# Re-ordered queues around latent attention, and the second block's scores as three products of rounded parts

## The reference, cut to what matters

```python
h = x
for i in range(2):
    h = h + (mla_mixer if i == 0 else gla_mixer)(rms_norm(h, ...))
    h = h + peer_ffn(rms_norm(h, ...), ...)
# second block, on rms_norm of h:
#   eight "neighbourhood" heads a (queries, keys, values of 64 each) and eight
#   "window" heads b with two key/value heads; q and k are rms-normed per head
s = einsum('qd,kd->qk', q, k) * 64 ** -0.5 + bias      # 256 x 256 per head
o = softmax(s) @ v                                      # heads b with a sink
h = h + (sigmoid(gate_a) * (o_a @ w_a) + sigmoid(gate_b) * (o_b @ w_b)) @ w_out
h = h + ffn(rms_norm(h))
```

## Time and profile before

| | |
|---|---|
| median of 3 runs | 2199.15 us (2199.08 to 2201.77) |
| profiled execution, its own time | 2194.29 us |
| its span, first to last instruction | 2192.6 us |
| PE busy | 2155.4 us, 98% of the span |
| DVE, ACT, POOL busy | 1555.7, 1246.0, 701.0 us |
| mean granted PE clock | 0.996 of full |
| latent attention | from 0 to about 135 us |
| second block up to its first scores | about 1808 to 1868 us |
| its 16 heads | 1868 to 1953 us |

### The profile page before, as it was taken

How to read it: one execution, slowest core, us unless ns; L and a number is a source line. 1 busy time by engine, 2 the same in 40 slices (tenths; PEclk the granted TensorE clock), 3 DMA queues, 4 the chain that set the end, 5 groups by cost and what they waited for, 6 DMA issues and landing times. The chain is left out here.

```text
span 2192.6 us, 35528 instructions
## 1 busy us (share of the span) xinstructions
PE 2155.4 (98%) x13161; PEld 1876.8 (86%) x13161; DVE 1555.7 (71%) x2944; ACT 1246.0 (57%) x2463; POOL 701.0 (32%) x340
## 2 busy tenths in 40 slices
PE   8899999999999999999999999999999999999999
PEld 8789998888888888887999888888888888887888
DVE  7658978888666666666698788866666669457776
ACT  6554577777455444564446777755545555555443
POOL 3217977777000000001698777720000004000000
PEclk9999999999999999999999999999999999999999
DMA  5144655555555555553555555555565557435554
GB/s 164 54 158 157 197 176 166 164 164 165 191 193 194 196 194 194 161 168 107 174 192 183 164 164 165 165 182 195 195 193 193 192 163 241 124 99 165 191 192 153
DMA packets 122956, 375.34 MB, mean 171 GB/s; under 512 B 13200, under 2 KB 18064, under 8 KB 122784
## 3 DMA queue, kind: packets, MB, share of 16 engines
q1 hardware_dynamic: 122352, 372.69, 52.6%
q10 hardware_dynamic: 432, 0.37, 0.0%
HBM read 371.96 MB, written 1.05 MB: 170 GB/s over the span
## 5 line engine op out<-in xcount | busy, mean ns | idle before, releaser
L250 ACT ACTIVATE hi<-raw 128x1024 fp32r<-128x1024 f32 (+2 forms) x705 | 738.0, 1048 | 365.9 <-PE bank L1424 113.6
L259 DVE TENSOR_TENSOR lo<-raw,hi 128x1024 fp32r<-128x1024 f32 (+2 forms) x445 | 537.3, 1211 | 266.0 <-ACT hi L250 265.6
L259 POOL TENSOR_TENSOR lo<-raw,hi 128x1024 fp32r<-128x1024 f32 (+1 forms) x260 | 628.9, 2423 | 222.4 <-ACT hi L250 222.0
L1465 PE MATMUL bank<-hi,pe_mh 128*128 128x512 f32 x1016 | 395.9, 390 | 1.3 <-DVE pe_ml L1719 1.3
L1466 PE MATMUL bank<-hi,pe_ml 128*128 128x512 f32 x1016 | 395.3, 389 | 0.0
L1413 PE MATMUL bank<-xx,hi 128*128 128x512 f32 x1176 | 308.9, 401 | 0.0
L1578 ACT ACTIVATE pe_mh<-pe_hidden 128x256 fp32r<-128x256 f32 x256 | 106.9, 418 | 341.9 <-PE bank L1472 341.9
L342 POOL TENSOR_TENSOR rstd<-mean,minus_half 128x2 f32<-128x2 f32 x6 | 4.2, 703 | 920.8 <-DVE mean L335 920.8
L1424 PEld LDWEIGHTS bank<-xx,lo 128*128 128x128 f32 x2048 | 269.4, 188 | 13.9
L1424 PE MATMUL bank<-xx,lo 128*128 128x256 f32 x2048 | 280.5, 280 | 0.0
L1472 PE MATMUL bank<-lo,pe_mh 128*128 128x512 f32 x1016 | 271.6, 389 | 0.0
(11 more groups left out here) (404 smaller groups left out, 3372.0 us busy)
## 6 DMA issues: line engine op xcount, KB each, us to landing
raw<-in_peer_u SPq DMA_DIRECT2D x256, 512.0 KB, 3.3
raw<-in_peer_v SPq DMA_DIRECT2D x256, 512.0 KB, 3.4
raw<-in_w_gate_up SPq DMA_DIRECT2D x44, 512.0 KB, 3.7
raw<-in_w_in SPq DMA_DIRECT2D x34, 512.0 KB, 4.4
raw<-in_gla_w_in SPq DMA_DIRECT2D x24, 512.0 KB, 3.6
raw<-in_w_down SPq DMA_DIRECT2D x22, 512.0 KB, 3.4
raw<-in_w_query SPq DMA_DIRECT2D x16, 512.0 KB, 3.3
raw<-in_mla_w_o SPq DMA_DIRECT2D x8, 512.0 KB, 3.3
```

The lines of the kernel that those rows point to most:

```text
L250: act.activation(k.hi[:, n % RING, at_hi:at_hi + x * e], k.raw[:, n % RAW, 0:x * e], ACT.Copy).then_inc(k.hi_done, 1)
L259: eng.tensor_tensor(k.lo[:, n % RING, at_lo:at_lo + x * e], k.raw[:, n % RAW, 0:x * e], k.hi[:, n % RING, at_hi:at_hi + x * e].bitcast(F32 ...
L1465: pe.matmul(second_ps(a, c), mh[:, v % 2, tok], hi[:, r, half], start=(v == 0), stop=False)
```

## The change

The diff is cut to what matters; the parts left out repeat those shown. In the latent attention, queues are re-ordered: DVE takes the sum, the mean and the copies of x before the angles, ACT copies x before it splits slab 0, fewer warming products run, POOL makes the low part of slab 3, `gain_rows` moves behind the low part of slab 6, POOL's turning of the mask goes behind its slabs 8 and 9, and a few steps in the loop over heads swap places. In the second block, each normed piece is written to `root` (which it reads), ACT rounds it into a high part and POOL subtracts for the low part; roots 2 to 5 now wait for that subtraction and stand in other turns of the loop; scores become three products.

```diff
@@ mla @@
+            add_slab(k, rows_of(w, 2 * b, 2, c0, width), 2, width, k.lo_pool if c0 and b else k.lo_dve,
...
-                keep_warm(k, pe, 2, 11)
+                keep_warm(k, pe, 2, 8)
                 pe.wait_ge(x_up[0].sem, x_up[0].at(16))
                 norm.given_raise(pe, 0)
-                keep_warm(k, pe, 2, 5)
+                keep_warm(k, pe, 2, 2)
                 pe.wait_ge(x_up[1].sem, x_up[1].at(16))
                 norm.given_raise(pe, 1)
-                keep_warm(k, pe, 2, 4)
+                keep_warm(k, pe, 2, 3)
...
                 split_lo(k, pool, 2)
+                split_lo(k, pool, 3)
+                split_lo(k, pool, M_UP)
+                split_lo(k, pool, M_UP + 1)
                 pool.wait_ge(mask_up.sem, mask_up.at(16))
                 pool.tensor_scalar(nmask[:], nmask[:], -1.0, None, ALU.mult).then_inc(neg_up.sem, 1)
-                split_lo(k, pool, M_UP)
-                split_lo(k, pool, M_UP + 1)
...
+                norm.keep_act(act)
                 split_hi(k, act, 0)
-                norm.keep_act(act)
+                norm.high(act, 0, 2)
                 split_hi(k, act, 1)
-                norm.high(act, 0, 2)
+                norm.high(act, 2, 4)
                 split_hi(k, act, 2)
-                norm.high(act, 2, KD)
-                for g in range(3):
-                    split_hi(k, act, g + RING)
-                act.wait_ge(reduced.sem, reduced.at(1))
-                act.activation(cs[:], cs[:], ACT.Sin).then_inc(sined.sem, 1)
-                split_hi(k, act, 6)
+                norm.high(act, 4, KD)
+                split_hi(k, act, 3)
+                split_hi(k, act, 4)
                 act.wait_ge(k.eaten, M_Q)
                 act.activation(csq[:, 3:5].rearrange("p j t -> p (j t)"), k.bank[0][:], ACT.Square).then_inc(c_sq.sem, 1)
+                split_hi(k, act, 5)
...
+                split_hi(k, act, 6)
+                split_hi(k, act, 7)
+                act.wait_ge(reduced.sem, reduced.at(1))
+                act.activation(cs[:], cs[:], ACT.Sin).then_inc(sined.sem, 1)
...
                     if i == 7:
                         keep_keys(5)
+                    if i == 8:
                         split_hi(k, act, 21)
                     if i == 9:
-                        split_hi(k, act, 22)
                         square_keys(3)
                         high_out(0)
+                        keep_values(3)
+                        split_hi(k, act, 22)
...
+                dve.wait_ge(x_up[1].sem, x_up[1].at(16))
+                norm.given_sum(dve, junk)
+                norm.mean(dve)
+                norm.keep_dve(dve)
+                dve.wait_ge(cols_up.sem, cols_up.at(16))
+                norm.low(dve, 0, 2)
+                split_lo(k, dve, 0)
+                norm.low(dve, 2, KD)
                 angles()
+                split_lo(k, dve, 4)
                 turned_angles(0)
+                split_lo(k, dve, 5)
                 turned_angles(1)
                 dve.sem_inc(reduced.sem, 1)
...
-                split_lo(k, dve, 3)
-                split_lo(k, dve, 4)
+                split_lo(k, dve, 6)
                 gain_rows()
+                low_lat(3)
+                low_lat(4)
+                split_lo(k, dve, 7)
@@ second_block @@
         def made_to(j):
+            return root[:, j % 2] if j < 6 else kbt[:, j - 6]
...
                     for a in range(NT):
-                        last = pe.matmul(s_ps(i)[:, a * T:(a + 1) * T], q_of(i)[:, a * P:(a + 1) * P], k_of(i),
-                                         start=True, stop=True)
+                        tok, ps = slice(a * P, (a + 1) * P), s_ps(i)[:, a * T:(a + 1) * T]
+                        pe.matmul(ps, q_of(highs, i)[:, tok], k_of(highs, i), start=True, stop=False)
+                        pe.matmul(ps, q_of(highs, i)[:, tok], k_of(lows, i), start=False, stop=False)
+                        last = pe.matmul(ps, q_of(lows, i)[:, tok], k_of(highs, i), start=False, stop=True)
...
@@ second_block, POOL @@
+                def split_made(j):
+                    pool.wait_ge(qk_hi.sem, qk_hi.at(j + 1))
+                    pool.tensor_tensor(part_of(lows, j), made_to(j), part_of(highs, j).bitcast(F32), ALU.subtract)\
+                        .then_inc(qk_lo.sem, 1)
+                split_at = (4, 6, 9, 10, 14, 14, 15, 15)
...
@@ second_block, ACT @@
+                def split_made(j):
+                    if j < 7:
+                        act.wait_ge(divided.sem, divided.at(j + 1))
+                    else:
+                        act.wait_ge(kb_done.sem, kb_done.at(1))
+                    act.activation(part_of(highs, j), made_to(j), ACT.Copy).then_inc(qk_hi.sem, 1)
                 def take_root(j):
                     act.wait_ge(meaned.sem, meaned.at(j + 1))
-                    if j >= 2:
-                        act.wait_ge(divided.sem, divided.at(j - 1))
+                    if 2 <= j < 6:
+                        act.wait_ge(qk_lo.sem, qk_lo.at(j - 1))
...
+                split_at = (AK + 3, BQ + 1, BKV, BKV + 1, AV + 2, AV + 3, GA, GA + 1)
+                root_at = (BQ + 1, BQ + 2, BKV + 1, AV)
...
-                    if g in (AQ + 4, AK + 4, BQ + 4):
-                        take_root(g // 4 * 2 - 2)
-                        take_root(g // 4 * 2 - 1)
+                    if g == AQ + 4:
+                        take_root(0)
+                        take_root(1)
+                    if g in split_at:
+                        split_made(split_at.index(g))
+                    if g in root_at:
+                        take_root(root_at.index(g) + 2)
...
+                        if i == H_A + 2:
+                            high_out(0)
                         if i < N_HEADS:
                             power(i)
-                        if i == H_A + 2:
-                            high_out(0)
@@ second_block, DVE, ahead of split_lo and of the two products with the gates @@
+                    if g == BA + 1:
+                        dve.wait_ge(raised.sem, raised.at(1))
+                        link(dve.tensor_tensor(total[:, H_A:], total[:, H_A:], esink[:], ALU.add))
+                        normalise(1)
```

More of the change, by code:

```diff
@@ L362, in keep_dve @@
                .then_inc(self.kept_dve.sem, 1)
-            if n == 0:
+            if n == 0 and not self.given:
                 self.mean(dve)
@@ L540, in _ @@
                 sp.dma_start(k.cols[:], k.dram["cols"]).then_inc(cols_up.sem, 16)
-                for n in range(AHEAD):
+                for n in range(RAW):
                     load_slab(k, sp, n)
-                sp.dma_start(nmask[:], k.dram["causal"]).then_inc(mask_up.sem, 16)
-                for n in range(AHEAD, M_SLABS + AHEAD):
+                at_freq, _ = ROWS["freq"]
+                with k.nc.allow_non_contiguous_dma(reason="narrow rows"):
+                    sp.dma_start(k.rows[:, 0:at_freq], k.dram["rows"][:, 0:at_freq]).then_inc(rows_up.sem, 16)
+                for n in range(RAW, M_SLABS + AHEAD):
                     load_slab(k, sp, n)
+                    if n == M_UP:
+                        sp.dma_start(nmask[:], k.dram["causal"]).then_inc(mask_up.sem, 16)
             @block.tensor
@@ L938, in _ @@
                 act.activation(krt[:], k.bank[1][0:ROPE, 0:T], ACT.Copy).then_inc(kr_out.sem, 1)
-                for n in range(7, 10):
+                split_hi(k, act, 6)
+                split_hi(k, act, 7)
+                act.wait_ge(reduced.sem, reduced.at(1))
+                act.activation(cs[:], cs[:], ACT.Sin).then_inc(sined.sem, 1)
+                for n in range(8, 10):
                     split_hi(k, act, n)
@@ L2304, in second_block @@
     with ExitStack() as ctx:
-        qt = k.sb(ctx, "sb_qt", [P, 4, T])
-        kt = k.sb(ctx, "sb_kt", [P, 4, T])
-        qbt = k.sb(ctx, "sb_qbt", [P, 4, T])
         kbt = k.sb(ctx, "sb_kbt", [P, 2, T])
+        highs, lows = ([k.sb(ctx, f"sb_{x}_{part}", [P, n, T], F32R) for x, n in (("qt", 4), ("kt", 4), ("qbt", 4), ("kbt", 2))]
+                       for part in ("hi", "lo"))
         va = k.sb(ctx, "sb_va", [P, NT, A_W])
@@ L2330, in second_block @@
         inv = k.sb(ctx, "sb_inv", [P, N_HEADS, NT])
-        made = ((qt, 0, 0), (qt, 1, 0), (kt, 0, 1), (kt, 1, 1), (qbt, 0, 2), (qbt, 1, 2), (kbt, 0, 3))
+        gain_of = (0, 0, 1, 1, 2, 2, 3)
         def made_ps(j):
@@ L2338, in made_to, with root_of @@
         def made_to(j):
-            dst, x, _ = made[j]
-            return dst[:, 2 * x:2 * x + 2].rearrange("p c t -> p (c t)") if j < 6 else kbt[:, 0]
+            return root[:, j % 2] if j < 6 else kbt[:, j - 6]
         def wide(j):
             return 512 if j < 6 else T
+        def root_of(j):
+            return root[:, j % 2] if j < 6 else sq[:, 0, T:2 * T]
         def half(h):
@@ L2349, in key_head, with part_of, q_of, k_of @@
             return h // (H_B // KV_B)
[L2351 to L2355 removed]
+        def part_of(of, j):
+            if j >= 6:
```

(17 more changed lines are left out.)

38 lines of the change are left out of this document (16 added, 22 removed).

## The result

The changed kernel took 2212.18 us, the median of 5 runs (2209.89 to 2214.09), beside 2201.77 us (2199.08 to 2204.27) of the kernel before: a ratio of 1.0049, 95% interval 1.0033 to 1.0065. In a later measurement it took 2209.73 us beside 2199.10: 1.0051 (1.0037 to 1.0065). It is slower by 10.5 us, where the forecast was 2.7. The new profiled execution took 2213.0 us, its span is 2211.3 us.

What follows compares the result with a forecast made beforehand. PE was taken to bound the kernel, busy 2155.4 of 2192.6 us. Terms of -5.9 - 3.2 + 9.5 - 0.4 - 0.3 + 3.0 = +2.7 us on 2199.15 gave 2202 us, range 2194.5 to 2209.

Steps and rivals of the forecast that it cites:

- rival "slower": Waits for roots 2 and 4, each followed by a full stretch at 1.2 GHz: about 2206 us, chance 0.37.
- scores: Second block: three products take 0.69 us a head instead of 1.06, over 16 heads, -5.9 us.
- outputs: Second block: earlier output split on ACT and normalisation on DVE remove two PE waits of 1.6 us, -3.2 us.
- waits for the roots and division 6: Second block: PE waits 3.6 us for slab 12, 3.8 for slab 16, 2.4 for division 6; +9.5 us.
- clock behind the root pauses: Second block: PE's clock likely falls behind the pauses for slabs 12 and 16, priced 1.2 and 0.7 us.
- start, loop and the clock there: Latent attention: early start nearly returned (-0.4 us), loop -0.3, clock behind the pause at the start +1.1.
- My lower bound, the hand-over paid twice: Smallest score gain allowed for: 0.22 us a head, -3.6 us, if the hand-over to the transposition doubles.
- the prediction's sum by it: Four passes for FP32: two full-width products take 8 x 0.113 = 0.90 us, gain only 3.6 us; not adopted.
- The chain of eight chunks on DVE: Start of latent attention: chunks of about 0.85 us each beside POOL delay slabs 1 to 3; slab 3 ends at 20.7.
- The row of steps behind it: From slab 3's end to the gains, 5.3 us with the hand-over; PE stands 3.4 us, transposes gains at 26.3.
- bounds of the clock: New pauses of PE: clock loss from nothing up to 5.1 us each; the range takes these in on both sides.

Runs made afterwards that it cites:

- Early roots: Changed kernel with roots 2 to 5 back at g = 8 and 12, copies and subtractions of the pieces moved ahead: 2201.73 us, ratio 1.0006.

## Why the prediction was wrong

The forecast was +2.7 us, a difference too small to tell; it is +10.5, and the time is beyond the upper end of the range. The direction is that of the rival "slower", and its mechanism, waits for the roots with the half clock behind them, is the one that the runs show for the larger part. But its 5 to 8 us fall short too, since it kept the gain of 5.9 us for the scores and a start that costs nothing.

| term | forecast | shown |
|---|---|---|
| scores | -5.9 | -1.6 to -1.9 (full-width against three products) |
| outputs | -3.2 | -3.3 (moved alone) |
| waits for the roots and division 6 | +9.5 | +8.6 and +8.9 (two profiles, less the 0.5 of before) |
| clock behind the root pauses | +1.9 | +4.5, give or take 3.5 (pauses filled) |
| start, loop and the clock there | +0.4 | +3.5 (alone), interval 1.1 to 6.2 |

The right column sums to some 11.6 us, against 10.5 measured; the intervals of its last two rows cover the difference.

- **Scores: the largest step that failed.** "Six of them take 0.68 us, and the hand-over to the transposition stays" carried the spacing of long rows of equal products over to six products of another shape. The rows show 0.22 us from the first to the second and 0.20 to the transposition, together 0.90 us, so the gain is 0.155 a head, 2.5 us in all. My lower bound, the hand-over paid twice, was 0.22 a head and did not hold it either. Another 0.6 to 0.9 us is lost in the other products of a head, which take some 0.05 us a head longer; why, no run shows. The Trainium skill, "FP8 and Floating Point Precision", TensorE Precision Notes, gives four passes to true FP32; the prediction's sum by it, 0.90 us for the full-width pair, does not agree with the 1.06 that the kernels with such a pair show. But that sum had no hand-overs either: two more steps of 0.12 us on top of the 0.90 of six products would be 1.14, an estimate from these rows, so they neither bear the rule out nor refute it. That its gain of 3.6 us lies nearer to the measured one than mine is no support for it.
- **The start.** "The chain of eight chunks on DVE (about 0.85 each with POOL beside it)" had the price for a chunk beside POOL, but not for two subtractions of DVE that each wait for one of POOL: 1.59 and 1.63 us. Slab 3's end slipped by 1.4 us, the gains with it. The row of steps behind it took nearly the time forecast (5.7 us from slab 3's end to the gains, 26.3 - 20.7 = 5.6 forecast, although the steps written out there sum to 5.3 only). The loop gave nothing back either, where 0.3 us was forecast: from its first to its last score it takes 58.9 us in both profiles of the kernel after, and 58.4 to 58.9 in those with the old order. That the pair of subtractions is what made slab 3 late is read from the trace; no run took POOL's out of the way. The Trainium skill, "SBUF — State Buffer", SBUF: two separate sides, says that a VectorE operation with two SBUF inputs and a GpSimd operation that reads SBUF lock each other out for the whole instruction. The trace agrees: DVE's starts behind POOL's, and 12.86, where POOL's ends, plus 0.62 us is 13.48, where DVE's ends; in the kernel before, where the same subtraction of DVE started ahead of POOL's, it took 0.75 us, and POOL's took 1.76 us instead of 1.42.
- **Waits for the roots.** Right in place, cause and size. The chain written out in the prediction gave 3.6, 3.8 and 2.4; the profile has 3.3, 3.8 and 1.9.
- **Clock behind them.** Undersized, 1.2 and 0.7 where up to 3.4 us each are at stake (half of 6.8) and some 4.5 together were found. "A fall is likely but not sure" was the error: in all five profiles that have the pauses unfilled, both falls are there and 6.8 us long.
- **Outputs.** Right; nothing else was late next.
- Three of five terms missed to the same side. The range had added up bounds of the clock, but the error of the scores, 4 us alone, lay outside the bounds that went into its upper end.

The main reason for the loss is one: ACT takes roots 2 to 5 one or two turns late. Early roots alone bring the changed kernel back to within 1.3 us (-0.7 to +3.5) of the kernel before. The new start is the smaller, second one.

## What to carry to other kernels

A short run of small products should be priced with both of its hand-overs, to the first product and to whatever follows, not at the spacing of a long run of equal ones. When a step moves back by a turn on one engine, add the wait it causes and, on PE, half the time that the clock will stand at half behind it; two or three pauses of 3 us are enough for most of a gain to vanish. And when a subtraction on DVE starts beside one on POOL, price the two in a row.

## What was not expected of the hardware

- Behind the same pause at the start the half clock lasted 10.2 us in two profiles and 3.4 us in three; behind the two root pauses it was 6.8 us each in all five profiles that have them unfilled. A stretch at half clock in one profile doesn't price a pause.
- Filling a pause removed the half clock behind it in both places, but only for the roots did the time move by more than its scatter.
- Single stretches of 3.4 us at half clock also stand where no edit reaches. Between 130 and 1800 us the first profile of the kernel after has none, its second has one, and that of early roots has three, worth some 5 us (half of 10.2). Effects of 2 to 4 us therefore need many runs, or distances read within a stage.
- 64-row products followed one another at 0.12 us, but the step from the first of them to the second took 0.22 us and the step back to the 128-row transposition 0.20, about 0.1 us more each.
